# GpSimd's subtraction of each weight tile issued as four instructions of 256 columns

## The chip, the cores and the metric

The kernel runs on one core of one Trainium2 chip. The metric is the device time of one execution in microseconds (us). One execution was taken by the hardware profiler; its span runs from the first to the last instruction.

## The reference

Two transformer blocks over 256 tokens of width 1024, in float32: an mLSTM mixer with an MLP and a gated embedding, then a block that joins forgetting attention with an RWKV-7 recurrence and ends in a product-key expert layer (PEER). Every weight matrix is read once and multiplied with the activations of all 256 tokens. The part that reads most weights is PEER, whose two tables have 128 x 128 experts of width 1024:

```python
h = jax.nn.gelu(jnp.einsum('thkd,td->thk', u_table[idx], xb), approximate=False)
return jnp.einsum('thk,thkd->td', gate * h, v_table[idx])
```

The kernel computes it densely: all 16384 experts for all tokens, with a gate that is zero for the experts not chosen.

## The kernel before

All weights are laid out by the host as 438 tiles of 128 partitions x 1024 float32 columns (`COUNTS`, in the order of use: qk 8, v 8, o 8, mix_out 8, w1 32, w2 32, ple_gate 8, ple 2, rwkv 14, fox_qk 8, fox_v 4, gates 16, p_fox 4, p_rwkv 4, w_o 8, peer_q 16, keys 2, u 128, v_table 128). They go through a ring of four slots (`RING`), each slot having a buffer in `RAW`, `WH` and `WL`.

A tile passes through five hands. SyncE loads it into `RAW` (L272), once the subtraction of the tile four places earlier is done (semaphore `w_lo`). ScalarE casts `RAW` to the rounded matmul type and writes `WH` (L357, and L684 inside loops), once the tile has landed and TensorE is through with the tile four places earlier (`w_used`). GpSimd then writes the remainder, `WL = RAW - WH` (L337), after waiting for the cast (`w_hi`), and reports on `w_lo`. TensorE waits for `w_lo` and takes the tile in one of two forms: `form_b` and `u_body` issue 24 matmuls of 256 columns for it, `form_a` and the `v_table` items 12 matmuls of 512 columns. Each product is made of three matmuls (high x high, high x low, low x high). The last matmul of a tile reports on `w_used`. So ScalarE and GpSimd run up to four tiles ahead of TensorE, never more.

VectorE takes no part in the weights' way, but works beside it. Three stretches matter here:

- The first 64 `u` tiles (called u1 below) run beside VectorE's top-k search of PEER, with several operations on 2048 columns of two tensors (L1724, L1727).
- During the last 64 `u` tiles (u2) VectorE makes one-hot rows for the gate matmuls, eight operations on 128 columns per tile (`hot_i` L1756, `hot_j` L1757), in groups that TensorE waits for after each tile, and takes the product out of PSUM with two more (`HS` L1771, `stage` L1773).
- During the 128 `v_table` tiles VectorE makes the low part of the activation, `CL = HS - CH` (L1785), once for each tile, and TensorE waits for it. During the first 64 of them (V1) it also multiplies gates fetched from HBM, two operations on 512 columns for each four tiles (`gate_rest`, L1779). The last 64 are called V2.

GpSimd does nothing else after its constants, which it makes in the first 14 us.

Of the kernel before, what the change touches and what calls it, by code (L numbers as in the profile page):

```python
# [19 lines left out]
ALU = mybir.AluOpType  # L20
# [83 lines left out]
def bass_blocks(nc, weights, x_in, p_in, vec_in, rows_in, gate_w_in, lora_in, mb_in, fb_in, out, rest_dram, x2_dram):  # L104
    with ExitStack() as ctx:
# [3 lines left out]
        def at(name, shape, dt, offset):  # L109
            return nc.alloc_sbuf_tensor_at(name, shape, dt, offset=base + offset)  # L110
# [5 lines left out]
        RAW = at("RAW", [P, RING, D], F32, 24576)  # L116
        WH = at("WH", [P, RING, D], F32R, 40960)
        WL = at("WL", [P, RING, D], F32R, 57344)
# [124 lines left out]
        def sem(name):  # L243
            if name not in sems:
                sems[name] = ctx.enter_context(nc.semaphore(name))
            return sems[name]

        w_landed = [sem(f"w_landed{i}") for i in range(RING)]
        w_hi, w_lo, w_used = sem("w_hi"), sem("w_lo"), sem("w_used")
# [5 lines left out]
        def plain(ap):  # L255
            return ap.bitcast(F32)
# [4 lines left out]
        @block.sync  # L261
        def _(sp):
            sp.dma_start(H[:, :, :], x_in.rearrange("(t p) d -> p t d", p=P)).then_inc(sem("x_landed"), 16)
            for n in range(RING):
                sp.dma_start(RAW[:, n, :], weights[n]).then_inc(w_landed[n], 16)
            full = (N_ITEMS // RING) * RING
            with sp.Fori(1, N_ITEMS // RING) as i:
                for slot in range(RING):
                    n = i * RING

                    sp.wait_ge(w_lo, n + (slot + 1 - RING))
                    sp.dma_start(RAW[:, slot, :], weights[bass.ds(n + slot, 1)].rearrange("a p d -> p (a d)")).then_inc(w_landed[slot], 16)  # L272
            for n in range(full, N_ITEMS):
                sp.wait_ge(w_lo, n + 1 - RING)
                sp.dma_start(RAW[:, n % RING, :], weights[n]).then_inc(w_landed[n % RING], 16)
            for t in range(NT):
                sp.wait_ge(sem("y_ready"), t + 1)
                sp.dma_start(out[t * P:(t + 1) * P, :], H[:, t, :]).then_inc(sem("y_stored"), 16)
            sp.wait_ge(sem("y_stored"), 16 * NT)


        @block.gpsimd
        def _(pool):
            made = sem("pool_made")
            count = [0]

            def link(ins):

                count[0] += 1
                ins.then_inc(made, 1)  # L290
                pool.wait_ge(made, count[0])

            def keep(view, pattern, base, cm, op, fill=0.0):
                link(nc.gpsimd.affine_select(out=view, in_=view, compare_op=op, fill=fill, base=base,
                                             pattern=pattern, channel_multiplier=cm))

            link(nc.gpsimd.memset(ident[:, :], 1.0))
            keep(ident[:, :], [[-1, P]], 0, 1, ALU.is_equal)
            nc.gpsimd.memset(ones_row[:, :], 1.0).then_inc(sem("ident_ready"), 1)
            link(nc.gpsimd.memset(sel4[:, :, :], 1.0))  # L300
            keep(sel4[:, :, :], [[-1, MH], [0, P]], 0, 1, ALU.is_equal)
            link(nc.gpsimd.memset(sel8[:, :, :], 1.0))
            keep(sel8[:, :, :], [[-1, FH], [0, P]], 0, 1, ALU.is_equal)

            link(nc.gpsimd.memset(mask_m[:, :, :, :], 1.0))
            for sb in range(NT):
                keep(mask_m[:, 0, sb, :], [[1, S]], -sb * P, -1, ALU.is_ge)
                keep(mask_m[:, 1, sb, :], [[-1, S]], sb * P, 1, ALU.is_ge)

            link(nc.gpsimd.memset(mask_f[:, :], 0.0))  # L310
            keep(mask_f[:, :], [[-1, S]], P, 1, ALU.is_ge, NEG)

            link(nc.gpsimd.memset(mask_r[:, :], 1.0))
            for half in range(2):
                v = mask_r[64 * half:64 * half + 64, :]
                keep(v[:, 0:64], [[1, 64]], -1, -1, ALU.is_ge)
                keep(v[:, 64:128], [[1, 64]], 0, -1, ALU.is_ge)
            link(nc.gpsimd.memset(blk_ones[:, :], 0.0))
            link(nc.gpsimd.memset(blk_ones[0:64, 0:64], 1.0))
            link(nc.gpsimd.memset(blk_ones[64:128, 64:128], 1.0))  # L320
            link(nc.gpsimd.memset(blk16[:, :], 1.0))
            for half in range(2):
                v = blk16[64 * half:64 * half + 64, :]
                keep(v, [[-BLK, 64 // BLK], [0, BLK]], 0, 1, ALU.is_ge)
                keep(v, [[BLK, 64 // BLK], [0, BLK]], BLK - 1, -1, ALU.is_ge)
            link(nc.gpsimd.memset(resets[:, :], 1.0))
            link(nc.gpsimd.memset(resets[:, :].rearrange("p (c t) -> p c t", t=CH_T)[:, :, 0:1], 0.0))
            link(nc.gpsimd.iota(iota_f[:, :], [[1, P]], base=0, channel_multiplier=0,
                                allow_small_or_imprecise_dtypes=True))
            link(nc.gpsimd.memset(eps_c[:, 1:2], GN_EPS))  # L330
            nc.gpsimd.memset(eps_c[:, 0:1], 1.0).then_inc(sem("consts_ready"), 1)

            def split_low(n, slot):


                pool.wait_ge(w_hi, n + 1)  # L336
                nc.gpsimd.tensor_tensor(WL[:, slot, :], RAW[:, slot, :], plain(WH[:, slot, :]),  # L337
                                        ALU.subtract).then_inc(w_lo, 1)

            full = (N_ITEMS // RING) * RING  # L340
            with pool.Fori(0, N_ITEMS // RING) as i:  # L341
                for slot in range(RING):
                    split_low(i * RING + slot, slot)
            for n in range(full, N_ITEMS):
                split_low(n, n % RING)
# [1546 lines left out]
```

## Time and profile before

| | |
|---|---|
| median of 3 runs | 1708.04 us (1705.97 to 1708.44) |
| span of the profiled execution | 1704.4 us |
| PE (TensorE matmuls) busy | 1554.7 us, 91% |
| DVE (VectorE) busy | 1056.9 us, 62% |
| ACT (ScalarE) busy | 749.9 us, 44% |
| POOL (GpSimd) busy | 1096.2 us, 64% |
| mean granted TensorE clock | 0.950 of full speed |

The time of the profiled execution itself is given only as its span; the median of the runs is 3.6 us above it. Busy time counts an instruction from its reported start to its reported end. That includes the time in which an instruction has begun and is held up, which matters for DVE and POOL here. Start times in the rows are us from the start of the span. "Idle before" is the time in which the engine had nothing running before an instruction, and the arrow names what released it.

### The profile page before, as it was taken

Reading aid. Unit: us, or ns where it says so; the run is one execution under the profiler, and the core shown is the slowest. Engines: PE = TensorE matmul, PEld = TensorE weight load, DVE = VectorE, ACT = ScalarE, POOL = GpSimd, SP = SyncE. Lnnn points to the kernel's source line nnn. Section 1 sums busy time; section 2 is a strip of 40 time slices with the busy share of each in tenths; the row PEclk is TensorE's granted clock in tenths of the full one; section 3 lists DMA queues with packets and bytes.
Section 4 is the critical chain, followed back from the end, with each engine's and each line's share of the span. In section 5 each row is a group of like instructions: output and inputs, shape, how many; then the busy total and the mean of one; then the engine's idle time right before and its main releaser. Section 6 shows DMA issues by size and latency. Waiting matters only on the chain.

```text
span 1704.4 us, 28276 instructions
## 1 busy us (share of the span) xinstructions
PE 1554.7 (91%) x9610; PEld 1372.4 (81%) x9610; DVE 1056.9 (62%) x1761; ACT 749.9 (44%) x1063; POOL 1096.2 (64%) x474
## 2 busy tenths in 40 slices
PE   6987999987998889878999998999999899999997
PEld 6765998866976679667999998888888777778885
DVE  3243451015729442243199906999999799978886
ACT  5344554344474323234466663223232444445443
POOL 7824788855858000155699985555555788878884
PEclk9988999998999669988999999999999999999998
DMA  4522455534534000134455454444444677665552
GB/s 171 184 74 99 138 185 191 193 123 130 182 121 158 27 1 13 38 125 159 139 183 185 160 197 143 142 153 148 147 141 149 228 232 229 220 205 193 196 189 95
DMA packets 74644, 254.99 MB, mean 150 GB/s; under 512 B 8409, under 2 KB 8793, under 8 KB 74330
## 3 DMA queue, kind: packets, MB, share of 16 engines
q1 hardware_dynamic: 63632, 231.76, 41.3%
q10 hardware_dynamic: 10954, 22.43, 3.9%
q8 instruction: 40, 0.66, 0.2%
q14 instruction: 18, 0.15, 0.0%
HBM read 243.67 MB, written 10.49 MB: 149 GB/s over the span
## 4 chain that ended last, share of the span: by engine, by line
issue 41%; POOL 25%; PE 20%; DVE 10%; DVEq 2%; DMA 1%; POOLq 1%; ACT 0%; ACTq 0%
POOL WL L337 24%; PE PS L783 20%; DVE hot_j L1757 4%; DVE hot_i L1756 4%; DVE CL L1785 1%; DMA stage<-gates_rest 1%; DVE HS L1779 1%; DVE HS L1771 0%; DVE stage L1773 0%; DVEq L1756 0%; DVEq L1757 0%; POOLq L341 0%; POOLq L336 0%; DVEq L1753 0%; DVEq L1771 0%
## 5 line engine op out<-in xcount | busy, mean ns | idle before, releaser
L337 POOL TENSOR_TENSOR WL<-RAW,WH 128x1024 fp32r<-128x1024 f32 x438 | 1084.4, 2484 | 585.6 <-ACT WH L357 385.8
L783 PE MATMUL PS<-XH,WH 128*128 128x256 f32 x1648 | 473.7, 287 | 4.3 <-POOL WL L337 2.2
L783 PE MATMUL PS<-XL,WH 128*128 128x256 f32 x1648 | 467.3, 284 | 0.0
L783 PE MATMUL PS<-XH,WL 128*128 128x256 f32 x1648 | 467.1, 283 | 0.0
L684 ACT CAST WH<-RAW 128x1024 fp32r<-128x1024 f32 x252 | 264.8, 1051 | 454.7 <-PE PS L783 451.1
L783 PEld LDWEIGHTS PS<-XH,WH 128*128 128x128 f32 x1648 | 317.4, 193 | 6.2 <-issue 2.6
L783 PEld LDWEIGHTS PS<-XL,WH 128*128 128x128 f32 x1648 | 317.3, 193 | 0.0
L783 PEld LDWEIGHTS PS<-XH,WL 128*128 128x128 f32 x1648 | 317.0, 192 | 0.0
L1785 DVE TENSOR_TENSOR CL<-HS,CH 128x256 fp32r<-128x256 f32 x128 | 267.6, 2113 | 41.7 <-ACT CH L718 41.7
L357 ACT CAST WH<-RAW 128x1024 fp32r<-128x1024 f32 x186 | 194.1, 1050 | 154.5 <-PE PS L783 150.2
L783 PE MATMUL PS<-WH,CH 128*128 128x512 f32 x512 | 201.7, 394 | 15.2 <-DVE CL L1785 15.2
L783 PE MATMUL PS<-WL,CH 128*128 128x512 f32 x512 | 200.7, 392 | 0.0
L783 PE MATMUL PS<-WH,CL 128*128 128x512 f32 x512 | 200.5, 392 | 0.0
L1756 DVE TENSOR_SCALAR hot_i<-iota_f,IT 128x128 f32<-128x128 f32 x256 | 169.7, 663 | 46.8 <-issue 42.8
L783 PEld LDWEIGHTS PS<-WH,CH 128*128 128x128 f32 x512 | 97.0, 190 | 38.0 <-DVE CL L1785 14.5
L783 PEld LDWEIGHTS PS<-WH,CL 128*128 128x128 f32 x512 | 97.0, 189 | 20.6
L1757 DVE TENSOR_SCALAR hot_j<-iota_f,JT,GT 128x128 f32<-128x128 f32 x256 | 113.2, 442 | 0.0
L783 PEld LDWEIGHTS PS<-WL,CH 128*128 128x128 f32 x512 | 97.1, 190 | 19.9
L1150 PE MATMUL PS<-hot_j,hot_i 128*128 128x128 f32 x512 | 89.7, 298 | 17.9 <-DVE hot_j L1757 15.1
L783 PE MATMUL PS<-WH,XH 128*128 128x512 f32 x240 | 97.3, 405 | 5.6 <-POOL WL L337 5.6
L1150 PEld LDWEIGHTS PS<-hot_j,hot_i 128*128 128x128 f32 x512 | 67.2, 191 | 37.3 <-DVE hot_j L1757 36.4
L783 PE MATMUL PS<-WL,XH 128*128 128x512 f32 x240 | 95.5, 398 | 0.0
(366 smaller groups left out, 1921.1 us busy)
## 6 DMA issues: line engine op xcount, KB each, us to landing
RAW<-weights SPq DMA_DIRECT2D x438, 512.0 KB, 3.4
gates_rest<-stage ACTq DMA_DIRECT2D x32, 256.0 KB, 3.7
stage<-gates_rest ACTq DMA_DIRECT2D x32, 256.0 KB, 3.1
H<-x SPq DMA_DIRECT2D x1, 1024.0 KB, 5.3
LG<-rows ACTq DMA_DIRECT2D x2, 512.0 KB, 4.8
LB<-rows ACTq DMA_DIRECT2D x2, 512.0 KB, 6.2
x<-H ACTq DMA_DIRECT2D x1, 1024.0 KB, 3.9
H<-x ACTq DMA_DIRECT2D x1, 1024.0 KB, 6.1
```

The costliest lines, as they stand in the source:

```text
L337: nc.gpsimd.tensor_tensor(WL[:, slot, :], RAW[:, slot, :], plain(WH[:, slot, :]), ALU.subtract).then_inc(w_lo, 1)
L357: nc.scalar.copy(WH[:, slot, :], RAW[:, slot, :]).then_inc(w_hi, 1)
L684: nc.scalar.copy(WH[:, slot, :], RAW[:, slot, :]).then_inc(w_hi, 1)
L783: last = mm(dst, a, b, start=start and k == 0, stop=stop and k == len(pairs) - 1)
L1150: last = mm(PS[:, 4 + c, k * NK:(k + 1) * NK], hot_i[:, g, a, :], hot_j[:, g, a, :], start=True, stop=True)
L1756: V.tensor_scalar(hot_i[:, g, a, :], iota_f[:, :], at_token(IT, t), None, ALU.is_equal)
L1757: last = V.tensor_scalar(hot_j[:, g, a, :], iota_f[:, :], at_token(JT, t), at_token(GT, t), ALU.is_equal, ALU.mult)
L1779: V.tensor_tensor(hs, hs, stage[:, b, :, :], ALU.mult).then_inc(sem("rest_gated"), 1)
L1785: V.tensor_tensor(CL[:, c, :], hs, plain(CH[:, c, :]), ALU.subtract).then_inc(sem("cl_ready"), 1)
```

## The change

The one instruction over 1024 columns becomes four over 256 columns each, one behind the other with no wait between them. The wait for the cast stands ahead of the first, and only the last reports on `w_lo`. The same columns are computed with the same operands. No other engine's program is touched.

```diff
                 pool.wait_ge(w_hi, n + 1)
-                nc.gpsimd.tensor_tensor(WL[:, slot, :], RAW[:, slot, :], plain(WH[:, slot, :]),
-                                        ALU.subtract).then_inc(w_lo, 1)
+                for part in range(4):
+                    k = slice(256 * part, 256 * part + 256)
+                    last = nc.gpsimd.tensor_tensor(WL[:, slot, k], RAW[:, slot, k], plain(WH[:, slot, k]),
+                                                   ALU.subtract)
+                last.then_inc(w_lo, 1)
```

## Rows read from the trace of the kernel before

In rows 4 the engines are PE, PEld, DVE, ACT and POOL, in this order.

**Rows 1.** The page's first part: busy time of an engine, share, instructions.

```profile
PE 1554.7 (91%) x9610; PEld 1372.4 (81%) x9610; DVE 1056.9 (62%) x1761; ACT 749.9 (44%) x1063; POOL 1096.2 (64%) x474
```

**Rows 2.** The page's chain that ended last: shares of the span by line.

```profile
POOL WL L337 24%; PE PS L783 20%; DVE hot_j L1757 4%; DVE hot_i L1756 4%; DVE CL L1785 1%; DMA stage<-gates_rest 1%; DVE HS L1779 1%; DVE HS L1771 0%; DVE stage L1773 0%; DVEq L1756 0%; DVEq L1757 0%; POOLq L341 0%; POOLq L336 0%; DVEq L1753 0%; DVEq L1771 0%
```

**Rows 3.** Tile WL: its writer (ns min/median/max), what ended GpSimd's idle time.

```profile
L337 POOL TENSOR_TENSOR WL<-RAW,WH x438: 2336/2402/4457, 14.5 to 1682.0; 128x1024 fp32r<-128x1024 f32 x146
...
  ACT WH L357: 385.8, 147
  ACT WH L684: 199.4, 192
```

**Rows 4.** Windows: stretch, its length, engines busy (instructions), clock, DMA share, GB/s.

```profile
14.00:98.00 84.00, 76.83 (x445) 66.08 (x444) 22.70 (x36) 36.47 (x44) 64.91 (x30) 0.98 0.49 162
180.00:355.00 175.00, 175.00 (x1118) 159.70 (x1116) 46.31 (x66) 84.63 (x130) 150.39 (x64) 1.00 0.57 188
485.00:557.00 72.00, 60.83 (x254) 46.88 (x252) 54.41 (x41) 41.29 (x50) 49.73 (x20) 0.95 0.42 139
852.00:1042.00 190.00, 185.01 (x1528) 184.21 (x1528) 135.70 (x404) 120.04 (x128) 172.71 (x65) 0.99 0.55 182
1042.00:1321.00 279.00, 265.08 (x2005) 245.62 (x2005) 275.33 (x619) 80.44 (x94) 150.21 (x62) 0.99 0.44 143
1325.00:1516.00 191.00, 178.32 (x770) 145.57 (x771) 175.58 (x100) 87.86 (x132) 163.98 (x64) 0.98 0.71 228
1516.00:1692.00 176.00, 175.69 (x767) 144.91 (x765) 138.82 (x61) 81.48 (x120) 143.63 (x60) 0.99 0.52 173
```

**Rows 5.** Timeline of GpSimd: one tile each of w2 and u1, two of u2.

```profile
285.54 2.39 POOL L337 TENSOR_TENSOR WL<-RAW,WH 128x1024 fp32r<-128x1024 f32 x1 [0.33 <-ACT WH L357]
...
858.44 2.41 POOL L337 TENSOR_TENSOR WL<-RAW,WH 128x1024 fp32r<-128x1024 f32 x1 [0.47 <-ACT WH L684]
...
1157.61 2.40 POOL L337 TENSOR_TENSOR WL<-RAW,WH 128x1024 fp32r<-128x1024 f32 x1 [2.15 <-ACT WH L684]
1161.96 2.39 POOL L337 TENSOR_TENSOR WL<-RAW,WH 128x1024 fp32r<-128x1024 f32 x1 [1.94 <-ACT WH L684]
```

**Rows 6.** Groups by form on GpSimd: count, busy us, mean ns, idle before.

```profile
L294 POOL TENSOR_SCALAR_AFFINE_SELECT mask_m<-mask_m 128x256 f32<-128x256 f32 x4 | 1.6, 398 | 0.3
...
L305 POOL MEMSET mask_m<- 128x1024 f32 x1 | 1.0, 956 | 0.1
...
L294 POOL TENSOR_SCALAR_AFFINE_SELECT ident<-ident 128x128 f32<-128x128 f32 x1 | 0.3, 292 | 0.1
...
L330 POOL MEMSET eps_c<- 128x1 f32 x1 | 0.1, 98 | 0.1
```

**Rows 7.** Timeline of GpSimd at the start: four tiles one behind the other.

```profile
14.45 9.40 POOL L337 TENSOR_TENSOR WL<-RAW,WH 128x1024 fp32r<-128x1024 f32 x4
```

**Rows 8.** Timeline of VectorE in u2, beside the last two of rows 5.

```profile
1157.74 2.35 DVE L1756 TENSOR_SCALAR hot_i<-iota_f,IT 128x128 f32<-128x128 f32 x1
1160.02 0.34 DVE L1757 TENSOR_SCALAR hot_j<-iota_f,JT,GT 128x128 f32<-128x128 f32 x1
...
1161.63 0.41 DVE L1771 TENSOR_TENSOR HS<-HS,PS 128x256 f32 x1
```

**Rows 9.** Timeline of both engines where V1 ends and in V2.

```profile
1504.11 2.65 POOL L337 TENSOR_TENSOR WL<-RAW,WH 128x1024 fp32r<-128x1024 f32 x1 [0.22 <-ACT WH L684]
...
1509.55 2.81 POOL L337 TENSOR_TENSOR WL<-RAW,WH 128x1024 fp32r<-128x1024 f32 x1
...
1529.66 2.39 POOL L337 TENSOR_TENSOR WL<-RAW,WH 128x1024 fp32r<-128x1024 f32 x1 [0.33 <-ACT WH L684]
...
1530.03 2.31 DVE L1785 TENSOR_TENSOR CL<-HS,CH 128x256 fp32r<-128x256 f32 x1 [0.41 <-ACT CH L718]
```

**Rows 10.** Groups on GpSimd in the stretch of u1 (852 to 1042).

```profile
L337 POOL TENSOR_TENSOR WL<-RAW,WH 128x1024 fp32r<-128x1024 f32 x65 | 174.2, 2701 | 14.3 <-ACT WH L684 14.3
```

## The prediction

> **What bounds the kernel now.** I read the busy times first. TensorE has work for 91% of the span, GpSimd for 64% [rows 1]. Yet the chain of work that ended last passes through the subtraction of L337 for 24% of the span, more than through any other line [rows 2]. So the subtraction is on or very near the path, although its engine is idle for a third of the time. The view of tile WL says why it may idle: nearly all of GpSimd's waiting, 385.8 + 199.4 us, ends with ScalarE's cast [rows 3], and that cast waits for TensorE to free a slot of the ring. GpSimd therefore follows TensorE wherever it can keep up.
>
> The windows and single tiles then show how near the two are. A tile takes GpSimd 2.40 us. In u1, with 24 matmuls per tile as in w1, 0.47 us of idleness stand before it, so TensorE's pace is 2.41 + 0.47 = 2.88 us. In w2 and V2, with 12 wide matmuls, it is 2.39 + 0.33 = 2.72 us [rows 5, 9]. The margins are 0.47 and 0.33 us a tile, and VectorE uses part of them, as follows.
>
> **The port that GpSimd shares with VectorE.** In u2 a one-hot operation on VectorE starts at 1157.74, after GpSimd's tile (1157.61), and takes 2.35 us. It ends 0.08 us after GpSimd's tile does, at 1160.09. The next such operations start 0.23 us apart on average: from 1160.02 to 1161.63 there are seven [rows 5, 8]. In V2 the subtraction of CL also begins inside GpSimd's tile and ends at 1532.34, 0.29 us after the tile's end at 1532.05 [rows 9]. So VectorE's operation is held until GpSimd's ends. It also works the other way: where GpSimd has its next tile ready at once, VectorE's waiting operation goes first and the tile then takes 2.65 us instead of 2.39, with one of 512 columns 2.81 [rows 9]. The two alternate, one instruction each. The Trainium skill (SBUF: State Buffer, section "Who interferes with whom") says that whoever issues first gets the shared pair for the whole instruction and the other fully blocks; the trace agrees, with the 2.35 us above.
>
> **The change part by part.** Nothing is removed: the same 1024 columns go through the same engine. Added are three more instructions a tile, 1314 in all, each with its fixed part. Their price is the first unknown, since the trace has L337 in one size only. GpSimd's constants give nearby rows. A memset, which reads nothing, takes 98 ns for one column and 956 for 1024, so 0.84 ns a column and 0.10 us fixed. An affine_select, which reads one operand, takes 292 ns for 128 columns and 398 for 256, so 0.83 ns a column and 0.186 us fixed [rows 6]. Going from no operand read to one adds 0.086 us to the fixed part. If the second operand of the subtraction adds as much again, the fixed part is 0.27 us. I take that, as the row it is nearest to is the one that reads and writes. The lower bound is the memset's 0.10. The upper bound is one more such step, 0.36, since the two operands come from two buffers.
>
> What counts is the time from start to start. Four tiles in a row take 9.40 us at the start, so (9.40 - 2.40) / 3 = 2.33 us from start to start for a duration of 2.40 [rows 7]. With durations from 2.34 (the smallest) to 2.40 [rows 3], 0.01 to 0.07 us of an instruction lie beside the one before it; I take 0.045. So an extra instruction costs 0.27 - 0.045 = 0.225 us. A tile costs 2.33 + 3 x 0.225 = 3.01 us, in pieces of about 0.80 us. With 0.10 fixed it would be 2.50 us, with 0.186 2.75, with 0.36 3.27.
>
> The Trainium skill (GPSIMD Engine Reference, section "Elementwise, side-by-side cycle accounting") gives 4497 ns for a tensor_tensor add of 2048 float32 columns. Against the 2402 ns here for 1024 [rows 3] that would make the fixed part an estimated 0.31 us, a tile 3.12 us, and the sum below 1874 us. No row here shows it.
>
> At 3.01 us GpSimd is slower than TensorE's 2.88 and 2.72. The ring hides some of that: when a stage begins with four tiles ready, GpSimd has about 4 us in hand. It has three tiles of TensorE's work (8.2 to 8.6 us) less one cast, its wait and one subtraction (1.2 + 3.0 us). Stage by stage:
>
> - qk, v and o (14 to 98): 24 tiles in a row, in which GpSimd is behind already. Sixteen are of the 2.72 kind: 16 x 0.29 = 5 us.
> - w1 and w2 (180 to 355): 64 tiles in 175 us without a gap, TensorE busy throughout [rows 4]. GpSimd's 60 tiles after the first four last 60 x 3.01 = 181 us, and TensorE's last tile 2.8 more: 183.5 - 175 = +8.5 us.
> - The gates (485 to 557): 16 tiles, GpSimd held by VectorE and catching up, 20 tiles in 72 us [rows 4]. Of 12 x 0.68 = 8 us I take 5 on the path, since attention's own chain follows.
> - mix_out, ple_gate, rwkv, fox, p_fox, p_rwkv, w_o, peer_q and keys: short stages or up to 26 tiles of small deficit, hidden by the ring. 1 us together.
> - u1 (852 to 1042): VectorE holds GpSimd up by (2.701 - 2.40) x 65 = 19.6 us [rows 10]. Today the margin of 0.47 x 60 swallows this. After the change it doesn't. GpSimd takes up its fifth tile at 858.4 [rows 5] and needs 60 x 3.01 + 19.6 = 200 us, TensorE 2.9 more: 1061 against 1036 (852 + 64 x 2.88). +25 us.
> - u2 (1042 to 1321): VectorE is busy for 275 of 279 us [rows 4], so it sets the pace, 4.35 us a tile (1161.96 - 1157.61). That is 2.40 held by GpSimd, seven further one-hot operations in 1.61 and one product of 0.33 [rows 5, 8]. With four pieces VectorE gets in one operation behind each. The last piece ends at 0.80 + 3 x (0.80 - 0.045 + 0.08) = 3.31 us. Then come four operations (0.92) and the product: 4.57 us. +0.22 x 62 = +14 us. So what VectorE gains by earlier access is less than the time that GpSimd stays longer.
> - V1 (1325 to 1516): per four tiles 4 x 3.01, four subtractions of CL that delay GpSimd by 0.26 each and two products by about 0.4 each: 13.9 us, 3.46 a tile, 221 us. TensorE has no work for 12.7 of the 191 us today [rows 4]; I take it that 5 of them, the handing over to V2, stay. That makes 226 against 191: +35 us.
> - V2 (1516 to 1692): 3.01 + 0.26 = 3.27 against 2.75 us a tile: +0.52 x 64 = +33 us.
>
> The sum is 5 + 8.5 + 5 + 1 + 25 + 14 + 35 + 33 = 127 us on a span of 1704.4, so 1831.5. The median of the runs is 3.6 us above the span: 1835 us. No wait is added. SyncE's loads are asked for by the last piece as before, later by 0.7 us. With a landing time of a few us and three tiles of time they stay hidden. TensorE will idle up to 0.5 us a tile. I expect no loss of clock: beside 8% of idleness at the start and 5% in u2 the granted clock was 0.98 and 0.99, and 0.95 beside 16% in the gates' stretch [rows 4]. Five per cent less clock makes 2.72 us 2.86, which still lies below 3.27.
>
> **The rivals.** First, smaller pieces are nearly free: GpSimd prepares the next one behind the running one, and the extra instruction costs 0.055 us (a fixed part of 0.10). Then a tile costs 2.50 us, below TensorE's pace in w1, w2 and u1. V2 stays at 2.76, V1 gets 2.95 a tile (+3). In u2 the last piece ends at 2.8 us and the pace is 4.07: -0.28 x 62 = -17 us. That gives 1694 us, faster. It decides from the point where u2's gain outweighs V, a fixed part of about 0.11. For it speaks that starts overlap at all [rows 7]. Against it stands the 0.186 of the nearest instruction that reads [rows 6].
>
> Second, the two operands are set up together, and the fixed part is 0.186. A tile costs 2.75: u2 even, w1 and w2 hidden, start 1, gates 2, u1 +10, V1 +19, V2 +16. That is 48 us, 1756 us.
>
> Third, GpSimd's pieces follow one another so closely that VectorE isn't let in between. Rows 9 speak against it, as there VectorE got in each time. Its operation would wait 3.0 us in u2, which makes 3.0 + 1.61 + 0.33 = 4.95 us a tile, +38 instead of +14: 1859 us. The upper bound of the fixed part, 0.36, gives by the same steps +9, +24, +8, +2, +41, +30, +51 and +50, 215 in all, 1923 us.
>
> **How the numbers follow.** The forecast (fixed part 0.23 to 0.31) has 0.55, the second rival 0.20, the first 0.12 (of it 0.08 faster by over 0.2% and 0.04 within). The third, with a still dearer piece, has 0.13. About 0.2% is what a measurement of this kernel can tell from no change. Slower has 0.55 + 0.20 + 0.13 = 0.88, same 0.04, faster 0.08. The range leaves out the first rival and the far end of the third: 1745 to 1880.
>
> **What would show it.** The group of L337 should have 1752 instructions of 128x256 with a median near 0.80 us, and about 0.75 from start to start where nothing interferes. In w1 GpSimd's idle time before a tile should be gone once the ring is empty, and TensorE should wait for WL. The subtraction of CL in V should fall from 2.31 us to below 1.2. hot_i in u2 should fall from 2.35 to below 1, while more of them are held. A median of 0.63 us in L337 would mean the first rival. Pieces of 0.80 with a total near 1710 would mean that the ring hides more than I reckon.

## The result and the profile after

| | before | after |
|---|---|---|
| median | 1707.97 us (1705.97 to 1708.44) | 1771.45 us (1758.78 to 1777.76) |
| span of the profiled execution | 1704.4 us | 1771.9 us |
| ratio | | 1.036, 95% interval 1.032 to 1.040 |

The change makes the kernel slower by 3.6%, 63.5 us. The forecast was 1835 us, 127 us slower: the right direction and twice the size. The nearest case on record is its second rival, 1756 us. In the experiments below, one execution of the kernel with whole tiles in u1 took 4434 us and is left out of its ratio; all others of a kernel lie within 20 us of one another.

The page of the changed kernel, first the busy times, then the shares by engine and by line of the chain that ended last (rows 1 and 2 answer to them):

```profile
PE 1575.4 (89%) x9610; PEld 1361.9 (77%) x9610; DVE 889.8 (50%) x1761; ACT 750.8 (42%) x1063; POOL 1309.2 (74%) x1788
...
POOL 55%; issue 29%; PE 12%; ACT 2%; DVE 1%; POOLq 1%; DVEq 0%; ACTq 0%
POOL WL L339 55%; PE PS L786 11%; POOLq L344 0%; ACT WH L360 0%; PE PS L775 0%; DVE H L1425 0%; PE PS L924 0%; PE PS L773 0%; DVE ST L1237 0%; ACT L390 0%; DVE H L1822 0%; DVE XS L1422 0%; DVE H L1431 0%; ACT LNS L635 0%; POOLq L336 0%
```

The subtraction (now L339; all lines below it have moved by 3) carries 55% of the chain instead of 24%. GpSimd is busy for 213 us more. VectorE is busy for 167 us less, because most of its operations are held for a shorter time.

Tile WL: the sizes of the writer (ns, least/median/most), which answer to rows 3.

```profile
L339 POOL TENSOR_TENSOR WL<-RAW,WH x1752: 712/740/2788, 14.4 to 1755.4; 128x256 fp32r<-128x256 f32 x195
```

A piece takes 0.740 us, not 0.80. The windows of the changed kernel, with the columns of rows 4 (start, w1 and w2, the gates, u1, u2, V1, V2; the bounds follow TensorE's work in this kernel):

```profile
14.00:97.00 83.00, 77.30 (x447) 65.12 (x446) 19.61 (x36) 37.22 (x44) 74.37 (x105) 1.00 0.48 154
173.00:361.00 188.00, 186.07 (x1157) 162.94 (x1156) 49.73 (x72) 88.46 (x135) 185.56 (x250) 1.00 0.52 171
498.00:570.00 72.00, 57.66 (x229) 43.31 (x227) 58.70 (x43) 38.29 (x47) 48.83 (x67) 0.88 0.37 122
864.00:1093.00 229.00, 189.62 (x1547) 188.83 (x1545) 183.78 (x414) 121.48 (x130) 193.24 (x263) 0.92 0.45 149
1093.00:1363.00 270.00, 257.49 (x2015) 244.12 (x2014) 268.84 (x629) 81.10 (x94) 176.06 (x249) 1.00 0.48 150
1367.00:1570.00 203.00, 187.57 (x768) 141.05 (x768) 80.41 (x95) 85.86 (x127) 197.14 (x247) 0.99 0.62 204
1571.00:1760.00 189.00, 186.14 (x768) 141.56 (x768) 45.89 (x67) 81.63 (x121) 185.12 (x248) 0.99 0.51 170
```

Against rows 4: u1 lasts 229 us instead of 190 (+39), u2 270 instead of 279 (-9), V1 203 instead of 191 (+12), V2 189 instead of 176 (+13). What lies ahead of u1 took 12 us longer (864 instead of 852). Together that is 67 us, as the two spans differ.

In V GpSimd works without a pause: 185.12 of 189 us in V2. In u1 something else happened. TensorE has 189.62 us of work in 229 us, so it stands still for 39 us, and its granted clock was 0.92 instead of 0.99. The waits of that stretch (engine and line, what it waited for, us in total, times, longest):

```profile
PEld PS L786 <- POOL WL L339: 37.0, 2, 33.4
ACT be L693 <- DVE be L1734: 36.0, 1, 36.0
POOL WL L339 <- ACT WH L687: 35.7, 1, 35.7
```

There is one long pause, of 33 us, and three engines share it. TensorE waits for GpSimd, GpSimd for ScalarE's cast, and ScalarE for the scores of VectorE's top-k. ScalarE needs them for an exponential (L693) that stands between its casts. VectorE is late with them because of three operations. The timeline of VectorE in u1:

```profile
881.36 18.05 DVE L1712 CAST tif<-ti 128x256 f32<-128x256 uint32 x1
899.33 2.82 DVE L1715 TENSOR_TENSOR cand<-tv 128x2048 f32<-128x2048 f32 x1
...
917.55 48.02 DVE L1720 TENSOR_SCALAR bai<-bp 128x128 uint32<-128x128 uint32 x1
965.50 0.78 DVE L1721 TENSOR_SCALAR bbi<-bp 128x128 uint32<-128x128 uint32 x1
...
1002.85 7.25 DVE L1712 CAST tif<-ti 128x256 f32<-128x256 uint32 x1
```

A shift of 128 columns took 48 us. In the kernel before, the same operation took 2.40 us:

```profile
884.46 2.40 DVE L1717 TENSOR_SCALAR bai<-bp 128x128 uint32<-128x128 uint32 x1
```

Beside the 48 us, GpSimd's timeline shows one chain of pieces without a gap, then the pause:

```profile
869.93 140.01 POOL L339 TENSOR_TENSOR WL<-RAW,WH 128x256 fp32r<-128x256 f32 x186
1045.60 4.83 POOL L339 TENSOR_TENSOR WL<-RAW,WH 128x256 fp32r<-128x256 f32 x7 [35.66 <-ACT WH L687]
```

VectorE waited while 69 pieces went by, though the next operation (0.78 us) was let in behind a single piece, as almost all are. Counted over the trace, of 507 operations of VectorE that began inside a piece with the next one directly behind, 502 were let in at the next boundary. Five waited on, for 3.3, 7.3, 18.1, 18.6 and 48.0 us, which is 5 to 69 pieces: passed over, as I call it below. In the kernel before, none of 45 was.

### The profile page after: what moved, and what is told of

Same layout as the page of the kernel before. It is cut to its first block, busy times and chain, and to the rows that moved or that the text cites. A ratio compares the mean times of both kernels' runs of the same rounds, so it can differ in the third digit from the quotient of the medians.

```text
span 1771.9 us, 29590 instructions
## 1 busy us (share of the span) xinstructions
PE 1575.4 (89%) x9610; PEld 1361.9 (77%) x9610; DVE 889.8 (50%) x1761; ACT 750.8 (42%) x1063; POOL 1309.2 (74%) x1788
## 4 chain that ended last, share of the span: by engine, by line
POOL 55%; issue 29%; PE 12%; ACT 2%; DVE 1%; POOLq 1%; DVEq 0%; ACTq 0%
POOL WL L339 55%; PE PS L786 11%; POOLq L344 0%; ACT WH L360 0%; PE PS L775 0%; DVE H L1425 0%; PE PS L924 0%; PE PS L773 0%; DVE ST L1237 0%; ACT L390 0%; DVE H L1822 0%; DVE XS L1422 0%; DVE H L1431 0%; ACT LNS L635 0%; POOLq L336 0%
## 5 line engine op out<-in xcount | busy, mean ns | idle before, releaser
L339 POOL TENSOR_TENSOR WL<-RAW,WH 128x256 fp32r<-128x256 f32 x1752 | 1297.6, 783 | 444.3 <-ACT WH L360 306.4
L786 PE MATMUL PS<-WH,CH 128*128 128x512 f32 x512 | 209.7, 410 | 21.9 <-POOL WL L339 14.9
L1788 DVE TENSOR_TENSOR CL<-HS,CH 128x256 fp32r<-128x256 f32 x128 | 94.9, 746 | 246.5 <-ACT CH L721 246.5
L1759 DVE TENSOR_SCALAR hot_i<-iota_f,IT 128x128 f32<-128x128 f32 x256 | 130.9, 511 | 44.5 <-issue 43.4
L1760 DVE TENSOR_SCALAR hot_j<-iota_f,JT,GT 128x128 f32<-128x128 f32 x256 | 141.7, 554 | 0.0
L786 PE MATMUL PS<-WH,XL 128*128 128x512 f32 x240 | 95.2, 397 | 0.0
```

The source lines that it names most:

```text
L339: last = nc.gpsimd.tensor_tensor(WL[:, slot, k], RAW[:, slot, k], plain(WH[:, slot, k]), ALU.subtract)
L786: last = mm(dst, a, b, start=start and k == 0, stop=stop and k == len(pairs) - 1)
L1759: V.tensor_scalar(hot_i[:, g, a, :], iota_f[:, :], at_token(IT, t), None, ALU.is_equal)
L1760: last = V.tensor_scalar(hot_j[:, g, a, :], iota_f[:, :], at_token(JT, t), at_token(GT, t), ALU.is_equal, ALU.mult)
L1788: V.tensor_tensor(CL[:, c, :], hs, plain(CH[:, c, :]), ALU.subtract).then_inc(sem("cl_ready"), 1)
```

## The experiments

Medians of the kernel before on the same chips lay between 1706.3 and 1707.2 us. Each kernel differs from the changed one or from the one before only in how GpSimd's loop issues a tile, unless said otherwise. The loop was cut at groups of four tiles, so that "u1" is tiles 184 to 247 and "u2" 248 to 311.

### Parts of the change alone, and one undone

Whole tiles in u1, four pieces elsewhere. The loop becomes three, and the last argument is the number of pieces. The other kernels of this kind differ in the bounds and numbers of pieces ("..." marks lines left out):

```diff
-            with pool.Fori(0, N_ITEMS // RING) as i:
+            with pool.Fori(0, 46) as i:
                 for slot in range(RING):
-                    split_low(i * RING + slot, slot)
...
+                    split_low(i * RING + slot, slot, 4)
+            with pool.Fori(46, 62) as i:
+                for slot in range(RING):
+                    split_low(i * RING + slot, slot, 1)
+            with pool.Fori(62, 109) as i:
+                for slot in range(RING):
+                    split_low(i * RING + slot, slot, 4)
```

> Four pieces everywhere but in the first 64 u tiles (tiles 184 to 247), which stay whole. My theory: in the changed kernel the 33 us in which TensorE has nothing to do inside that stretch come from VectorE operations of the top-k search (the cast of ti, the shift of bp) that GpSimd's gapless pieces passed over for 18, 48 and 7 us; ScalarE then waits 36 us for the scores and all its casts wait behind that. With whole tiles these operations take at most 2.5 us, the pause is gone, and the stretch falls back from 225 us to about 185: 1771 - 38 = 1730 to 1738 us. Rival: the pause comes from GpSimd's slower pace or from ScalarE's own order, and whole tiles give back only the pace, at most 6 us: 1765 us or more.

Measured: 1741.18 us, ratio 1.020 (1.018 to 1.022). That is 30 us less than the changed kernel. No operation of VectorE's top-k lasts more than the 4.4 us that the widest took before, and the pause is gone. From the first matmul of peer_q to the last of u1 TensorE takes 259 us, against 287 in the changed kernel and 248 in the one before. That is 11 us more than before, and the total is 3 us above my range. The profiled execution shows where 10 of the 11 us went. Just ahead of u1 TensorE ran at a lower granted clock. The window of those 20 us in this kernel:

```profile
838.00:858.00 20.00, 18.84 (x96) 18.65 (x96) 0.32 (x1) 2.60 (x3) 5.95 (x7) 0.56 0.28 94
```

The 96 matmuls of `keys` took 18.8 us there and 10.9 us in the kernel before, where the clock of that stretch was 1.00. What made it fall isn't shown. u1 itself began at the lower clock (0.73 from 858 to 870) and took 189.2 us, 2.3 more than before. So nothing is left for a slower pace.

Four pieces in u2 alone:

> Four pieces only in the last 64 u tiles (248 to 311), whole tiles elsewhere. My theory: there VectorE gets in one one-hot operation behind each piece at no cost to GpSimd's pace, so the stretch gets shorter by 11 us as in the changed kernel (280 to 269 us): 1697 us. Rival: the 11 us are an effect of how the stretch was entered (ring full, VectorE ahead) and of a lighter stretch before; then no difference, 1706 to 1709 us.

Measured: 1694.60 us, ratio 0.993 (0.992 to 0.994). That is 12 us less, and the gain in u2 stands by itself.

Four pieces in the v_table tiles alone:

> Four pieces only in the v_table tiles (312 on), whole tiles elsewhere. My theory: GpSimd's tile of 4 x 0.697 = 2.79 us and the subtraction of CL that gets in once per tile for 0.18 make 2.97 us against TensorE's 2.72: +16 us in the first half and +11 in the second, as in the changed kernel: 1735 us. Rival: VectorE's earlier access makes up for it and the loss was carried over from before: under 1715 us.

Measured: 1733.90 us, ratio 1.015 (1.014 to 1.017), +27 us. The two halves of V last 203 and 189 us, as in the changed kernel.

Four pieces in u1 alone:

> Four pieces only in the stretch of u1 (tiles 184 to 247), whole tiles elsewhere. My theory: a tile of 2.79 us with VectorE's 20 us of holding up is a little over TensorE's pace (0 to 6 us), and one or more of VectorE's three operations cast of ti, shift of bp, second cast are passed over by gapless pieces for tens of us, so that the scores come late and TensorE waits some 30 us: 1735 to 1750 us, with a spread between runs larger than that of the kernel before (5 us). Rival: the passing over needs what came before in the changed kernel (later phase, ring emptier); then 1708 to 1714 us.

Measured: 1745.09 us, ratio 1.023 (1.022 to 1.025), +39 us. The spread is 3 us, not larger than before. The same three operations are passed over: the two casts for 20.9 and 4.5 us, the shift for the same 48 us again. Timeline of VectorE in this kernel:

```profile
904.53 48.04 DVE L1725 TENSOR_SCALAR bai<-bp 128x128 uint32<-128x128 uint32 x1
```

Four pieces in all tiles before the u tiles:

> Four pieces in all tiles before the u tiles (0 to 183), whole tiles elsewhere: the part not yet tried alone. My theory: w1 and w2 lose 7 us as in the changed kernel and the stretch of the gates 7 to 10 us, because an operation of VectorE there is passed over too (18 us in the changed kernel), 16 to 20 us in all: 1722 to 1727 us. Rival: these losses were hidden or belong to one execution: under 1714 us.

Measured: 1711.70 us, ratio 1.004 (1.002 to 1.006), with single runs from 1708.4 to 1726.4. This is the rival's number: my range began at 1722. w1 and w2 do lose their 7 us (187.1 us of TensorE's stretch instead of 179.5), but part of it comes back in the following stages, and the loss in the gates' stretch isn't in the median. Two of ten runs lay at 1723 and 1726. In the profiled execution (span 1712.5) only the shortest of the five, the 3.3 us behind w2, was passed over, while the changed kernel's profile has an 18.6 us operation in the gates' stretch. That such an event makes the two long runs is likely, but those two have no trace.

The parts add up to 5 + 39 - 12 + 27 = 59 us, against the 63.5 measured for the whole. The 4.5 us between them may be that operation: TensorE's 20 tiles up to the end of the gates took 81.3 us in the changed kernel's profile and 76.6 in this one's.

### The price of a piece

Two pieces of 512 columns everywhere:

> Two pieces of 512 columns everywhere. By the sizes measured (1024 columns 2.40 us, 256 columns 0.74) a piece should take 1.29 us, 1.25 from start to start, and a tile 2.33 + 0.155 = 2.49 us, below TensorE's 2.88 and 2.72 and with CL still at 2.68. My theory (the loss comes from the tile's length beyond TensorE's pace and from what follows from a GpSimd without gaps): no operation of VectorE is passed over for more than 3 us, u2 gains a little, 1698 to 1710 us. Rival (each boundary between pieces costs as such, or VectorE is passed over wherever pieces follow one another): a third of the loss, 1725 us or more.

Measured: 1705.14 us, ratio 0.999 (0.998 to 1.000): no difference. Tile WL in this kernel:

```profile
L339 POOL TENSOR_TENSOR WL<-RAW,WH x876: 1259/1298/3451, 14.5 to 1681.1; 128x512 fp32r<-128x512 f32 x176
```

The piece is 1.298 us, as expected. Twice as many instructions cost nothing here, where the tile stays under TensorE's pace. Of 305 waiting operations of VectorE all were let in at the next boundary.

Eight pieces of 128 columns in u2 alone:

> Eight pieces of 128 columns in the last 64 u tiles only. By the two sizes measured (256 columns 0.74, 1024 columns 2.40 us) a piece should take 0.74 - 128 x 2.16 ns = 0.46 us, 0.42 from start to start, a tile 3.35 us. All eight one-hot operations then get in behind pieces. My theory (VectorE's order sets the pace: the length of GpSimd's tile plus what is left after it): 3.35 + 0.08 + 0.33 + 0.33 = 4.1 us a tile against 4.22 with four, 1687 to 1695 us. Rival: each piece's length is dominated by its fixed part and the tile gets longer than what it lets in, or SyncE's next load comes too late: 1700 us or more.

Measured: 1660.67 us, ratio 0.974 (0.972 to 0.975). The gain is 46 us, three times what I expected. The groups of GpSimd, then the window of u2, in this kernel:

```profile
L339 POOL TENSOR_TENSOR WL<-RAW,WH 128x128 fp32r<-128x128 f32 x512 | 220.7, 467 | 20.8 <-ACT WH L692 20.8
```

```profile
1036.00:1273.00 237.00, 237.00 (x2014) 236.82 (x2013) 225.39 (x626) 80.52 (x94) 215.96 (x496) 1.00 0.53 173
```

The tile did get longer for GpSimd, which is busy for 216 us in 237. But TensorE is now busy throughout. My model kept VectorE's two products of 0.33 us behind GpSimd's tile, one after the other. With eight pieces GpSimd works beside them, and they are not held: all 61 of each kind between 1040 and 1270 took 0.41 us with a piece running. The one-hot operations are held for 0.50 us at a time. Timeline of VectorE in this kernel:

```profile
1184.16 0.50 DVE L1764 TENSOR_SCALAR hot_i<-iota_f,IT 128x128 f32<-128x128 f32 x1
1184.58 0.50 DVE L1765 TENSOR_SCALAR hot_j<-iota_f,JT,GT 128x128 f32<-128x128 f32 x1
1185.00 0.50 DVE L1764 TENSOR_SCALAR hot_i<-iota_f,IT 128x128 f32<-128x128 f32 x1
```

So the stretch went from VectorE's pace (4.35 us a tile) to TensorE's (237 / 64 = 3.70 us).

Four pieces in u2 and two in V, then eight in u2 and two in V, whole tiles elsewhere:

> Whole tiles up to the first 64 u tiles, four pieces in the last 64 u tiles, two halves in the v_table tiles. My theory: the gains of the two earlier kernels add up: 1694.6 for four pieces in u2 alone, less 1 to 2 us in V where a tile of 2.49 us plus CL stays below TensorE's 2.72: 1692 to 1695 us. Rival: V is bound by TensorE in both and the halves only add risk: 1695 to 1700 us.

> Whole tiles up to u1, eight pieces of 128 columns in u2, two halves in the v_table tiles. My theory: the gain of eight pieces in u2 (1660.7) and the 1 us of halves in V add up: 1658 to 1661 us. Rival: the V part follows a faster u2 with a ring less full and loses it: 1662 to 1666 us.

Measured: 1693.59 us (0.993) and 1658.61 us, ratio 0.972 (0.970 to 0.973). The parts add up. The second is faster than both kernels of this case, by 2.8% than the one before.

### What VectorE's long waits hang on

Four pieces in u1 alone, each piece waiting for the one before it:

```diff
+                    if done is not None and part < parts - 1:
+                        last.then_inc(sem("piece"), 1)
+                        pool.wait_ge(sem("piece"), done + part)
```

> As the kernel with four pieces in u1 only, but there each piece waits until the one before it has finished, so that GpSimd is never gapless inside a tile. My theory: VectorE is passed over because the next piece has already begun when one ends; with the wait VectorE gets in at the next boundary every time, none of its operations lasts over 5 us, and TensorE's long pause is gone. The tile is longer, 4 x (0.74 + 0.06) = 3.2 us, which costs (3.2 - 2.88) x 60 + 10 = 20 to 30 us: 1728 to 1738 us. Rival: a waiting operation of this kind (one input, both ports) can be passed over at any boundary, gap or not; then operations of 10 us and more stay, and the time is 1750 us or more.

Measured: 1739.81 us, ratio 1.019 (1.018 to 1.021). No operation of the top-k lasts over 2.9 us and the long pause is gone. But the time is barely less than with the pause. The wait leaves 0.08 us between pieces, and the median tile takes 3.14 us from start to start. That is a little above my range.

Four pieces in u1 alone, one wait after each tile:

```diff
                 last.then_inc(w_lo, 1)
+                if finish:
+                    pool.wait_ge(w_lo, n + 1)
```

> Four pieces in u1 only, and after each tile GpSimd waits until its own last piece has finished; inside the tile the pieces still follow without a gap. My theory: VectorE is passed over without end only where the gapless chain runs across tiles; with one gap of 0.08 us a tile it is let in after three pieces at most, so no operation lasts over 5 us, and TensorE's pause of 33 us is gone. A tile takes 2.79 + 0.12 = 2.91 us: 1712 to 1722 us. Rival: one gap in four boundaries isn't enough, operations of 10 us and more remain: 1735 us or more.

Measured: 1737.33 us, ratio 1.017 (1.016 to 1.019). By its time this is my rival's number, and by its trace my theory's: all of 56 waiting operations were let in at the next boundary. What failed was the price of the wait. The timeline of GpSimd:

```profile
874.64 2.83 POOL L339 TENSOR_TENSOR WL<-RAW,WH 128x256 fp32r<-128x256 f32 x4 [0.45 <-POOL WL L339]
877.62 2.85 POOL L339 TENSOR_TENSOR WL<-RAW,WH 128x256 fp32r<-128x256 f32 x4 [0.16 <-POOL WL L339]
880.63 2.83 POOL L339 TENSOR_TENSOR WL<-RAW,WH 128x256 fp32r<-128x256 f32 x4 [0.16 <-POOL WL L339]
```

The gap is 0.16 us after a tile and 0.45 where the loop goes round, so a tile takes 2.83 + (3 x 0.16 + 0.45) / 4 = 3.06 us. With that, the sum of the prediction's u1 step (60 tiles, VectorE's 20 us and 2.9) gives 207 us from the fifth tile on, 29 more than TensorE's pace needs; measured +31.

The same wait in all tiles of the changed kernel:

> The changed kernel with that wait after each tile everywhere. My theory: the 33 us in u1 and the passing over in the gates' stretch go, while tiles of 2.91 instead of 2.79 us cost 0.12 x 128 = 15 us in V and about 6 in w1 and w2: 1745 to 1758 us, with runs closer together than the 19 us of the changed kernel. Rival: the wait only adds time, 1785 us or more.

Measured: 1800.46 us, ratio 1.055 (1.053 to 1.057). By the time the rival is right. The passing over is gone (none of 443 waiting operations waited for more than two pieces), but tiles of 3.06 us in every stage cost more than it did. The runs do lie closer together (9 us).

Four pieces in u1 alone, with ScalarE's wait for the scores four tiles later, and the same move in the kernel before:

```diff
-IJG_AT = NK // 8 - 2
+IJG_AT = NK // 8 - 1
```

> As the kernel with four pieces in u1 only (1745.1 us), but ScalarE's wait for the scores, its exponential and TensorE's transposes of the choice come one loop body, that is four u tiles or 11.5 us, later (IJG_AT 15 instead of 14). My theory: VectorE's scores are as late as before, 48 us of passing over included, and ScalarE's wait of 36 us, which holds back its casts, begins 11.5 us later and so lasts 24 us: TensorE's pause falls from 33 to about 22 us and the time to 1734 us. Rival: the pause is set by GpSimd's or VectorE's pace and not by where ScalarE waits: 1743 us or more.

> The kernel before with the same move and nothing else. There the scores are ready long before ScalarE asks. My theory: no difference, 1705 to 1709 us. Rival: the move costs something by itself, since the one-hot rows start later: 1712 us or more, which would have to be taken off the other kernel's time.

Measured: 1745.97 us and 1706.78 us. The move costs nothing by itself and it gives nothing back: the pause is 33 us as before. My theory of the pause fell here. The trace shows what it is. Timelines of VectorE and of GpSimd in the first of these kernels:

```profile
986.22 18.39 DVE L1717 CAST tif<-ti 128x256 f32<-128x256 uint32 x1
...
854.69 149.76 POOL L339 TENSOR_TENSOR WL<-RAW,WH 128x256 fp32r<-128x256 f32 x200
1040.11 32.51 POOL L339 TENSOR_TENSOR WL<-RAW,WH 128x256 fp32r<-128x256 f32 x42 [35.65 <-ACT WH L692]
```

The second cast ends at 1004.61, 0.16 us after GpSimd's chain, at 1004.45. Without the move it had ended at 994.34, 0.15 us after a chain that ended ten microseconds earlier (854.78 + 139.41 = 994.19). So in both kernels this cast is passed over until GpSimd has nothing left to do. GpSimd runs out only when ScalarE stops casting, and ScalarE stops only where it waits for the scores, which need this cast. VectorE then has the same work before it, about 36 us, wherever that wait stands. The place of the wait shifts the pause and doesn't shorten it.

One gap in GpSimd's chain for each four tiles:

```diff
+                if finish:
+                    pool.wait_ge(w_lo, n + 1)
...
+                    split_low(i * RING + slot, slot, 4, slot == RING - 1)
```

> Four pieces in u1 only, and GpSimd waits for its own last piece once in four tiles instead of after each. My theory: VectorE's waiting operation is let in at the next gap, so each of the three casts and shifts lasts 12 us at most; 30 us of lateness stay within the 43 us that the one-hot rows wait today, TensorE's pause of 33 us is gone. A tile takes 2.79 + 0.5 / 4 = 2.91 us, so 60 x 2.91 + 20 + 2.9 from 858.4 ends 20 us later than today: 1722 to 1730 us. Rival: one gap in sixteen boundaries does not let it in, operations of 18 us and more stay and so does the pause: 1745 us or more.

Measured: 1726.57 us, ratio 1.011 (1.009 to 1.013), inside my range. None of VectorE's casts and shifts lasts over 1.9 us, and the pause is gone. It costs half of what four pieces in u1 cost without the gap. The casts behaved as my theory has it: both were let in at a gap, the first after three pieces, the second, which began in the last piece before one, after 0.83 us. The first cast, then GpSimd beside it, in the timelines of this kernel:

```profile
869.94 1.89 DVE L1719 CAST tif<-ti 128x256 f32<-128x256 uint32 x1
...
867.46 4.22 POOL L339 TENSOR_TENSOR WL<-RAW,WH 128x256 fp32r<-128x256 f32 x6
872.13 3.19 POOL L339 TENSOR_TENSOR WL<-RAW,WH 128x256 fp32r<-128x256 f32 x2 [0.45 <-POOL WL L339]
```

The shift, the dearest of the three before, was let in at once (0.45 us) in the middle of a chain of sixteen pieces. The next gap was 13 us away, so the gap didn't let it in. It may be the place inside a tile at which an operation begins, which the gaps move too. In the three kernels where the three operations were passed over, they began at the same places each time: the first cast 0.24 to 0.26 us into the third piece of a tile, the shift 0.16 to 0.19 us into the fourth, the second cast 0.59 to 0.62 us into the second. With the gaps the first cast and the shift both began in the second piece. No run changes the place alone, and what decides at a boundary stays open.

## Why the prediction was half right

**The direction and its reason held.** A subtraction in four pieces is longer than TensorE's 2.72 us, and GpSimd becomes the bound in V. Rows 5 and 9 gave TensorE's pace before any run, and with four pieces in V alone the loss was 27 us.

**The term that was mis-sized is the fixed part of a piece.** I took 0.27 us by adding a step of 0.086 for the second operand. The sizes measured are 0.740, 1.298 and 2.40 us for 256, 512 and 1024 columns: 2.18 ns a column between the first two, 2.15 between the last, and a fixed part of 0.740 - 256 x 2.17 ns = 0.185 us. That is the affine_select's 0.186 of rows 6, the second rival's number. That the two agree may be chance, as their prices per column differ (0.83 and 2.17 ns), and the rival's reason, that both operands are set up together, is not shown. Taking off the 0.045 us that lie beside the instruction before, an extra piece costs about 0.15 us where I had 0.225. A tile is 2.33 + 3 x 0.15 = 2.78 instead of 3.01 us, and 128 tiles of V alone make 29 us of the error. The 4497 ns that the Trainium skill gives (GPSIMD Engine Reference, section "Elementwise, side-by-side cycle accounting") led by my estimate to 0.31 us; the 0.185 measured here is further from it than from my 0.27.

**The price of letting VectorE in was too high.** In u2 I added 0.08 us a piece. Four pieces last 2.83 us there, with VectorE's operations behind them:

```profile
1204.18 2.83 POOL L339 TENSOR_TENSOR WL<-RAW,WH 128x256 fp32r<-128x256 f32 x4 [1.52 <-ACT WH L687]
...
1204.92 0.77 DVE L1760 TENSOR_SCALAR hot_j<-iota_f,JT,GT 128x128 f32<-128x128 f32 x1
1205.62 0.78 DVE L1759 TENSOR_SCALAR hot_i<-iota_f,IT 128x128 f32<-128x128 f32 x1
```

The pieces come every 0.70 us with these operations behind them, as they do without, so the hand-over costs GpSimd nothing here. With a last piece at 2.83 instead of 3.31 us my own sum for u2 gives 4.09 us a tile. Measured were 4.25 (0.16 of it unexplained), below the 4.35 of before, hence -9 us in the changed kernel and -12 with u2 alone, instead of +14. For the subtraction of CL in V the 0.26 was 0.19: where it got in, the piece took 0.92 instead of 0.73 us.

**V** by the corrected terms: (2.78 + 0.19) x 64 = 190 us for V2, measured 189. The step was right but for its size: both halves of V together were forecast at +68 us and measured at +27 with four pieces there alone.

**w1 and w2** lost 8 us as forecast, but for another reason. With 2.78 us the ring should have hidden w1. VectorE holds GpSimd up there too. The group of GpSimd from 180 to 350 in the changed kernel:

```profile
L339 POOL TENSOR_TENSOR WL<-RAW,WH 128x256 fp32r<-128x256 f32 x228 | 170.5, 795 | 0.0
```

The pieces average 0.795 us instead of 0.740, which makes a tile 3.0 us. For this stretch I had counted no share of VectorE. The gates, +5 in the forecast, cost TensorE's 20 tiles 6 us in the changed kernel (81.3 instead of 74.9), but only 1.7 us (76.6) in the kernel in which no operation was passed over there. The start, +5 as well, lost nothing (its window ends at 97 instead of 98).

**u1 is where a mechanism was missing.** The forecast had +25 us from pace, and the sum had no term for an operation that is passed over. With four pieces in u1 alone TensorE's stretch from peer_q on grew from 247.7 to 286.8 us: 33 us of pause and 6 more. Of the 6, 3.7 are a second wait for the subtraction, and the rest is TensorE's clock behind the pause. The windows of the changed kernel, where it went the same way (before the pause, in it, after it):

```profile
1005.00:1015.00 10.00, 10.00 (x86) 10.00 (x85) 9.96 (x10) 1.70 (x2) 4.95 (x8) 1.00 0.47 157
1038.00:1048.00 10.00, 0.00 (x0) 0.00 (x0) 5.82 (x7) 5.19 (x6) 2.40 (x4) 0.50 0.00 0
1048.00:1058.00 10.00, 9.48 (x61) 9.49 (x62) 0.00 (x0) 6.37 (x8) 10.00 (x16) 0.73 0.52 162
1058.00:1068.00 10.00, 10.00 (x86) 10.00 (x86) 0.00 (x0) 6.03 (x9) 10.00 (x16) 1.00 0.62 204
```

After 33 us without work the granted clock was 0.50, the lower of its two levels (1.2 GHz), and TensorE began 61 matmuls in ten microseconds instead of 86, which is 2 to 3 us. So the pace itself cost under 4 us. My third rival had VectorE not let in between pieces, but in u2 and for the length of one tile, and I gave it little, because in rows 9 VectorE got in each time. That remains true of 502 cases in 507. Three of the five others were the dear ones, since a passed-over operation can be held for many tiles.

**The clock** held where GpSimd set the pace, as forecast: 0.99 in both halves of V. It did not hold elsewhere: 0.92 instead of 0.99 in u1 and 0.88 instead of 0.95 in the gates' stretch, where the forecast had expected no loss.

**That 1771 lies inside the range of 1745 to 1880 is luck.** Two errors work against each other: the piece was priced too high, and the pause was missing. Without the pause of 33 us the time would be about 1738, and whole tiles in u1 gave 1741, both below the range. The second rival's 1756 has the right piece, but the same luck: it had +35 us for V (measured +27), none for u2 (-12) and +10 for u1 (+39).

The forecast's signs were of use: the median in L339 tells a fixed part of 0.186 from the others at once, and the subtraction of CL (0.79 to 0.95 us) and hot_i (0.77) fell as far as forecast. The 0.63 us that it names for the first rival is wrong by its own terms, which give 0.67 (2.50 / 4 + 0.045).

## What to carry to other kernels

Where GpSimd and VectorE share a port, read first which of the two is waited for in each stage. Small pieces on GpSimd help where VectorE sets the pace and GpSimd has slack (eight pieces in u2: -46 us), and hurt where GpSimd's tile is near the pace of the engine that it feeds (V: +27 us). Take the price of a piece from a run with two sizes of the same instruction where you can (here 0.185 us and 2.17 ns a column), and compare pieces x (fixed + columns) with the pace, stage by stage. And don't let small pieces run without a gap for long beside a VectorE that others wait for.

## What the runs showed of the hardware that I had not expected

- An operation of VectorE waiting for the shared port was almost always let in behind the current piece (502 of 507 in the changed kernel). The others were passed over for 5 to 69 pieces, up to 48 us, while later ones got in at once. By more than two pieces it happened only with 256 columns, in a chain without a gap across tiles. It did not happen in the kernel with halves (305 cases) or in the one with eight pieces in u2 (372). Two of the five in the changed kernel got in only as GpSimd ran dry. The 48 us came out the same in three kernels (48.02, 48.04, 48.03), so it isn't chance alone. All passed-over operations of u1 in these three kernels (nine) got in behind the last piece of a tile, which is where GpSimd's program waits for the next cast, although 425 of the 502 ordinary ones began in the first three pieces of a tile and got in inside it. The 3.3 us case got in inside a tile too. What decides it is open.
- The rule that I cited from the Trainium skill (SBUF: State Buffer, section "Who interferes with whom"), that the one that issues first gets the shared pair for the whole instruction and the other blocks, agrees with the traces for a single instruction (2.35 us beside a tile in u2, 0.50 beside a piece of 128 columns). It does not bound the wait against a chain of them, which here reached 48 us.
- A GpSimd wait on its own last instruction leaves a gap of 0.08 us inside a tile, 0.16 after a tile and 0.45 where the loop goes round. Without a wait the next instruction begins 0.04 us before the last ends.
